# Sparse attention's gate projection: weights stationary instead of x, and its place among the first matmuls of the layer

## The chip, the core and the metric

The kernel runs on one core of one Trainium2 chip. The metric is the device time of one execution in microseconds (us). Engines are named as in the profile: PE is TensorE's matmuls and PEld its weight loads, DVE is VectorE, ACT is ScalarE, POOL is GpSimd, SP is SyncE, which here only issues DMAs.

## The reference, cut to what matters

A model of three blocks on 256 tokens of width 1024: the first has two mixers, cross attention and an FFN, the other two each an FFN, a mixer and an FFN. The mixer of the second block is sparse attention ("nsa"). Of it, this is what the change touches:

```python
hn = rmsnorm_2(x, mix_norm[layer])            # x: 256 tokens x 1024
...
q, kc, vc, ks, vs, kw, vw, gates = jnp.split(h @ w_in, splits, axis=-1)
...
g = jax.nn.sigmoid(gates.reshape(B, S, NSA_HKV, G, 3).transpose(0, 2, 3, 1, 4))
o = g[..., 0:1] * o_cmp + g[..., 1:2] * o_sel + g[..., 2:3] * o_win
```

`gates` are the last 48 columns of the 2608 of `w_in`: for each of 16 query heads three numbers per token, one for each of the three kinds of attention. Everything is float32.

## The kernel before, in words

**Layout.** The residual stream `HT` is kept transposed: the 1024 features in eight blocks of 128 partitions, the 256 tokens along the free axis. The input of a projection, x, is `XR`: the same eight blocks, scaled by the norm's gain, each split into a high part (rounded to the matmul's fp32r) and a low part (the rest). Weights come from memory in units of 2048 columns (eight k-blocks of 256 output features), and are split likewise into `WH` and `WL`. ScalarE writes the high part (L1152), VectorE the low part (L1737). There are three buffers for raw and three for split units. `mm2` (L511) makes one product of three matmuls: high times high, and the two mixed ones. The root of the mean square is not applied to x but afterwards, to the results (`scale`, L1770, on VectorE, with rows `RN`, or with a column per token).

**A unit.** `unit_T` (L536) computes a unit of 256 features: its weights are stationary (128 x 128), x moves (256 columns), and the result comes out transposed as features x tokens. It is 2 halves x 8 blocks x 3 = 48 matmuls. The gate is the exception (L966 to L973): its unit has 8 x 48 columns, and there x is stationary and the weights move, 48 columns at a time, so that the result has tokens on its partitions: 2 halves of the tokens x 8 blocks x 3 = 48 matmuls also. The later steps want it so: `gates` is a per-token, per-head factor (`settle_pair`, L1889, and the compressed part).

**Order.** Each engine runs a list written out by hand, and they meet at semaphores. The order around the change is, on TensorE: the last matmuls of the FFN's output; the gate (first the six blocks of x that are there, then the seventh and eighth; `in_order_of_x`, L532); the column sums for the norm (`norm_sum`, L588: two matmuls of 256 columns and four of 2, in a bank of their own); unit 6 (first keys, `("k", 0)`); unit 0 (first queries); the sum of squares of the first keys (`sum_squares`, L688, one float32 matmul of 512 columns, two in the records); unit 8; the next sum; unit 7; the next; and then the loop of `p` in 0 to 18 over pairs of heads (L997), in which each step has scores, transposes and weighted sums, with the other units between. Its last steps (about 932 to 966 us) are thin: small matmuls between exponentials and reductions.

On ScalarE (L1577 to L1600): the high part of unit 0 (`asked(("nsa_gate", 0))`, which looks three units ahead), the root of the mean square (`rsqrt_mean`, L1178, two operations), the high part of unit 8 (`asked(("nsa_w_in", 6))`), the gate's three steps (exponential twice, logarithm, exponential, L1582 to L1588), the squares of the first keys (`nsa_square`), the high part of unit 7, the root for them (`nsa_root`), and so on. A high part waits until the unit that held its buffer three before has been used: unit 8 follows the gate, unit 7 follows unit 6.

On VectorE (L2320 on): the low part of unit 0, `ncol`, the low part of unit 8, the scaling of the first keys, the low part of unit 7, the scaling of the first queries, and so on. The last block of x is written at L1745 (`chunk_lo`), after the FFN's last result has been added at L1795.

PSUM has eight banks. `take("main", ...)` goes round banks 0 to 2, `take("aux", ...)` round 4 to 7; each waits for the event named by `empties` of its former holder. `RS` is half of ScalarE's scratch, 512 columns; `in_bank` gives the bank of a key.

Of the kernel before, what the change touches and what calls it, by code (L numbers as in the profile page):

```python
# [194 lines left out]
def program(nc, A, out):  # L195
# [5 lines left out]
    ACT = mybir.ActivationFunctionType  # L201
# [4 lines left out]
    U = {name: u for u, (name, *_) in enumerate(UNITS)}  # L206
# [12 lines left out]
    with ctx:  # L219
# [3 lines left out]
        def signal(name, step=1):  # L223
            s = Signal(ctx.enter_context(nc.semaphore("s_" + name)), step)
            SIGNALS.append(s)
            return s
# [33 lines left out]
        SQ, RS, T2 = TMP[:, 0, :], TMP[:, 1, :], TMP[:, 2, :]  # L260
# [6 lines left out]
        used = signal("used")  # L267
# [10 lines left out]
        cmp_pe = signal("cmp_pe")  # L278
# [6 lines left out]
        copied = signal("copied")  # L285
        sig1 = signal("sig1")
# [16 lines left out]
        lo_done = signal("lo")  # L303
        parts = signal("parts")
        rscaled = signal("rscaled")
# [38 lines left out]
        def stat(name, n):  # L344
            if name not in stat_of:
                stat_of[name] = stat_at[0]
                stat_at[0] += n
                assert stat_at[0] <= 768, "STAT"
            return STAT[:, stat_of[name]:stat_of[name] + n]
# [6 lines left out]
        def tiles(ap, t):  # L356
            return ap.rearrange("p (k t) -> p k t", t=t)
# [11 lines left out]
        def con(name):  # L369
            at, n = CCOLS[name]  # L370
            return CON[:, at:at + n]

        def half(buf, n):
            return buf[:, n * 512:n * 512 + 512]

        def two(buf):
            return tiles(buf[:, 0, :], 256), tiles(buf[:, 1, :], 256)

        def split_at(u, cols):

            if u in IN_XR:
                return XR[:, 0, 0:cols], XR[:, 1, 0:cols]
            return WH[:, PART[u], 0:cols], WL[:, PART[u], 0:cols]
# [5 lines left out]
        ident, ones64, ones128 = con("ident"), con("ones64"), con("ones128")  # L389
# [67 lines left out]
        gates = stat("gates", 96)  # L457
# [5 lines left out]
        def in_bank(key):  # L463
            return banks[BANK[key]][:, :]
# [25 lines left out]
        def tensor(e, counting):  # L490
            q = Queue(e, counting)
# [5 lines left out]
            def take(kind, key):  # L497
                i = kinds[kind][turn[kind] % len(kinds[kind])]
                turn[kind] += 1
                for s, k in emptied.pop(i, ()):  # L500
                    q.wait_ge(s, k)
                BANK[key] = i
                return banks[i]

            def empties(key, *events):
                emptied[BANK[key]] = events

            def mm(o, l, r, start=True, stop=True):
                return e.matmul(o, l, r, start=start, stop=stop)  # L509

            def mm2(o, l, r, start, stop):  # L511
                mm(o, l[0], r[0], start, False)
                mm(o, l[0], r[1], False, False)
                return mm(o, l[1], r[0], False, stop)

            def at_k(x, k, a, n):
                return x[0][:, k, a:a + n], x[1][:, k, a:a + n]

            def weights(name, n=256, cols=2048):
                u = U[name]  # L520
                _, _, _, whole = UNITS[u]
                if whole:
                    q.wait_ge(raw[u % NRAW], u)
                    return u, tiles(RAW[:, u % NRAW, 0:cols], n)
                q.wait_ge(lo_done, u)
                return u, tuple(tiles(part, n) for part in split_at(u, cols))
# [5 lines left out]
            def in_order_of_x(m, k):  # L532

                return (0, m, k) if k < 6 else (k, m, k)

            def unit_T(name, x, x_name, pieces, *events, kind="main", order=in_time):  # L536
                u, w = weights(name)
                b = take(kind, name)
                for m, k in sorted(((m, k) for m in range(2) for k in range(8)), key=lambda mk: order(*mk)):
                    q.wait_ge(parts, (x_name, k * pieces // 8))  # L540
                    t = mm2(b[:, m * 256:m * 256 + 256], at_k(w, k, m * 128, 128), at_k(x, k, 0, 256), k == 0 and m == 0, k == 7 and m == 1)
                t.then_inc(used.tick(u), 1)
                empties(name, *events)
# [144 lines left out]
            def sum_squares(key, ones, *events, squares=SQ):  # L688
                b = take("aux", key)
                q.wait_ge(squared, key)  # L690
                mm(b[:, :], ones, squares).then_inc(summed.tick(key), 1)
                empties(key, *events)


            xT = two(XR)
# [192 lines left out]
            def nsa_unit(i, key, kind="one"):  # L888
                unit_T(("nsa_w_in", i), xT, "mix_0", 8, (rscaled, key), kind=kind)
# [12 lines left out]
            def nsa_sum(key):  # L902
                sum_squares(key, ones64, (ln_done, key))
# [59 lines left out]
                    t = mm(b[:, r * 256:r * 256 + 256], BDV[:, G, r, :], PCT[:, G, :], False, r == 1)  # L963
                t.then_inc(cmp_pe.tick(("out", G)), 1)

            name = ("nsa_gate", 0)  # L966
            u, w = weights(name, 48, 384)
            b = take("main", name)
            for j, k in sorted(((j, k) for j in range(2) for k in range(8)), key=lambda jk: in_order_of_x(*jk)):
                q.wait_ge(parts, ("mix_0", k))  # L970
                t = mm2(b[:, j * 48:j * 48 + 48], at_k(xT, k, j * 128, 128), at_k(w, k, 0, 48), k == 0 and j == 0, k == 7 and j == 1)
            t.then_inc(used.tick(u), 1)
            empties(name, (sig1, ("gate", 1)))  # L973
            norm_sum("mix_0")
            nsa_unit(6, ("k", 0), "main")
            nsa_unit(0, ("q", 0), "main")
            nsa_sum(("k", 0))
            nsa_unit(8, ("k", 1), "main")
            nsa_sum(("q", 0))
# [116 lines left out]
            for p in range(11):  # L1096
# [18 lines left out]
                if 0 <= p - 3:  # L1115
# [6 lines left out]
                    b = in_bank(("diff", "o", h // 2))  # L1122
# [15 lines left out]
        def scalar(e, counting):  # L1138
            q = Queue(e, counting)
# [14 lines left out]
            def asked(name, less=0):  # L1154
                ahead(U[name] + NW - less)
# [22 lines left out]
            def rsqrt_mean(stage):  # L1178

                n = 260 if stage in WITH_COLS else 256  # L1180
                b, r = in_bank(("norm", stage)), RN[stage][:, 0:n]
                q.wait_ge(small["con"], 0)
                q.wait_ge(ssq, stage)
                if stage == "ffn1_0":
                    e.activation(RR, b[:, 0:256], ACT.Ln, bias=eps, scale=0.125).then_inc(ln_done.tick("final"), 1)
                    q.wait_ge(ln_done, "final")
                    e.activation(r, RR, ACT.Exp, scale=-1.0).then_inc(rstd.tick("final2"), 1)
                    q.wait_ge(cols, "final")
                    e.activation(r, r, ACT.Ln, bias=eps, scale=0.125).then_inc(ln_done.tick("final2"), 1)
                    q.wait_ge(cols, "final2")  # L1190
                    e.activation(r, r, ACT.Exp, scale=-0.5).then_inc(rinv.tick(stage), 1)
                    e.activation(RR, RR, ACT.Exp, scale=-0.5).then_inc(rstd.tick("final"), 1)
                    return
                e.activation(r, b[:, 0:n], ACT.Ln, bias=eps, scale=0.125).then_inc(ln_done.tick(stage), 1)
                q.wait_ge(ln_done, stage)
                e.activation(r, r, ACT.Exp, scale=-0.5).then_inc(rinv.tick(stage), 1)
# [12 lines left out]
            def copy(key, dst, src):  # L1209
                e.activation(dst, src, ACT.Copy).then_inc(copied.tick(key), 1)  # L1210
# [10 lines left out]
            def rows_square(key, src, dst, former):  # L1221

                if former is not None:
                    q.wait_ge(summed, former)
                e.activation(dst, src, ACT.Square).then_inc(squared.tick(key), 1)
# [314 lines left out]
            def nsa_square(key):  # L1540
                q.wait_ge(rscaled, key)
                rows_square(key, half(QN, key[1]) if key[0] == "q" else (T2, KR1)[key[1]], SQ, FORMER_N[key] or ("ob2", 3))
# [33 lines left out]

            asked(("nsa_gate", 0))  # L1577
            rsqrt_mean("mix_0")
            asked(("nsa_w_in", 6))
            q.wait_ge(used, U[("nsa_gate", 0)])  # L1580
            q.wait_ge(cols, "ncol")
            for j in range(2):  # L1582
                e.activation(gates[:, j * 48:j * 48 + 48], in_bank(("nsa_gate", 0))[:, j * 48:j * 48 + 48], ACT.Exp,
                             scale=ncol[:, j:j + 1]).then_inc(sig1.tick(("gate", j)), 1)
            q.wait_ge(sig1, ("gate", 1))
            e.activation(gates, gates, ACT.Ln, bias=con("one")[:, 0:1]).then_inc(sig2.tick("gate"), 1)
            q.wait_ge(sig2, "gate")
            e.activation(gates, gates, ACT.Exp, scale=-1.0).then_inc(gated.tick("gate"), 1)  # L1588
            nsa_square(("k", 0))
            asked(("nsa_w_in", 0))  # L1590
            nsa_root(("k", 0))
            nsa_square(("q", 0))
# [1023 lines left out]
```

## Time and profile before

| | us |
|---|---|
| median of 3 runs | 1682.28 |
| lowest and highest of them | 1681.22, 1685.14 |
| the profiled execution | 1686.05 |
| its span in the profile | 1684.2 |
| PE busy, share of the span | 1652.2, 98% |
| DVE busy, share | 1095.1, 65% |
| ACT busy, share | 919.5, 55% |
| HBM read over the span | 281 MB, 167 GB/s |

The profile is of one execution. A matmul's length there contains the filling and emptying of the array, so matmuls that follow each other overlap; how long a run of them takes is read from the difference of starts. The granted clock is a share of TensorE's full speed: 1.00 is its level of 2.4 GHz and 0.50 its level of 1.2 GHz. Times in the text are counted from the span's start.

### The profile page before, as it was taken

To read this page: it belongs to the slowest core of one execution; us is meant where nothing else is said; L and a number is where in the kernel's file an instruction comes from. 1 tells how busy PE (TensorE), PEld (TensorE's weight loads), DVE (VectorE), ACT (ScalarE), POOL (GpSimd) and SP (SyncE) were. 2 spreads that over 40 slices of the span, in tenths; PEclk is the share of its full clock that TensorE was granted. 3 is DMA by queue.
4 is the path that set the end of the run, shared out by engine and by line. 5 is a ranking of instruction groups with operands and counts; after the bars stand their busy time and mean duration, and the time that the engine had idled before them with its cause. 6 is when DMAs were issued, how large, how long until landed. Compare 5 with 4: busy or idle time off the path is not lost.

```text
span 1684.2 us, 30435 instructions
## 1 busy us (share of the span) xinstructions
PE 1652.2 (98%) x13180; PEld 1566.1 (93%) x13180; DVE 1095.1 (65%) x1371; ACT 919.5 (55%) x1248; POOL 159.2 (9%) x63
## 2 busy tenths in 40 slices
PE   7999999999999999999999899999999999999999
PEld 7999989999999989998988699998999898799998
DVE  6888868664666567756578856656655667665554
ACT  6966778445444455434487844444443447754432
POOL 0000000000022101220000002210122000012210
PEclk9999999999999999999899899999999999999999
DMA  7555344454455455545542235545554564245543
GB/s 268 184 176 172 130 150 143 184 179 147 150 190 186 156 197 199 200 162 172 195 143 101 101 126 192 183 155 197 203 198 160 173 220 151 101 143 184 191 155 129
DMA packets 44629, 284.01 MB, mean 169 GB/s; under 512 B 4944, under 2 KB 6608, under 8 KB 17744
## 3 DMA queue, kind: packets, MB, share of 16 engines
q1 hardware_dynamic: 44352, 281.99, 48.0%
q8 instruction: 104, 1.70, 0.4%
q14 instruction: 29, 0.24, 0.0%
q10 hardware_dynamic: 144, 0.08, 0.0%
HBM read 281.00 MB, written 1.05 MB: 167 GB/s over the span
## 4 chain that ended last, share of the span: by engine, by line
PE 86%; DVE 6%; ACT 5%; issue 2%; DMA 1%; DVEq 0%; ACTq 0%
PE bank L509 85%; ACT WH L1152 2%; DVE WL L1737 2%; PE bank L660 1%; DVE HT L1793 0%; ACT SB L1275 0%; ACT XM L1159 0%; DVE XM L1745 0%; ACT XR L1159 0%; ACT FB L1176 0%; DVE FB L1763 0%; DVE STAT L1882 0%; DMA RAW<-in_nsa_w_out 0%; DMA PAR<-in_par 0%; DVE FA L2178 0%
## 5 line engine op out<-in xcount | busy, mean ns | idle before, releaser
L1737 DVE TENSOR_TENSOR WL<-RAW,WH 128x2048 fp32r<-128x2048 f32 (+1 forms) x282 | 590.3, 2096 | 272.2 <-ACT WH L1152 272.0
L509 PE MATMUL bank<-XR,WH 128*128 128x256 f32 x3648 | 651.2, 282 | 11.2 <-DVE WL L1924 10.7
L1152 ACT ACTIVATE WH<-RAW 128x2048 fp32r<-128x2048 f32 (+1 forms) x282 | 493.1, 1752 | 217.4 <-PE bank L509 211.2
L509 PEld LDWEIGHTS bank<-XR,WH 128*128 128x128 f32 x3648 | 559.7, 189 | 15.5 <-DVE WL L1924 10.7
L509 PE MATMUL bank<-XR,WL 128*128 128x256 f32 x1824 | 511.1, 280 | 0.0
L509 PEld LDWEIGHTS bank<-XR,WL 128*128 128x128 f32 x1824 | 344.4, 189 | 0.0
L509 PE MATMUL bank<-XF,WH 128*128 128x512 f32 x880 | 305.3, 392 | 0.0
L509 PE MATMUL bank<-XM,WH 128*128 128x256 f32 x1664 | 299.0, 282 | 3.3 <-DVE XM L1745 1.8
L509 PEld LDWEIGHTS bank<-XM,WH 128*128 128x128 f32 x1664 | 256.9, 190 | 4.8 <-DVE XM L1745 2.8
L509 PE MATMUL bank<-XF,WL 128*128 128x256 f32 x880 | 246.0, 280 | 0.0
L509 PE MATMUL bank<-XM,WL 128*128 128x256 f32 x832 | 234.2, 281 | 0.0
L509 PEld LDWEIGHTS bank<-XF,WH 128*128 128x128 f32 x880 | 165.2, 188 | 36.3
L2463 POOL TENSOR_TENSOR FA<-FA,R 128x512 f32<-128x512 f32 x33 | 92.2, 2794 | 859.7 <-ACT FA L1252 859.7
L509 PEld LDWEIGHTS bank<-XF,WL 128*128 128x128 f32 x880 | 165.2, 188 | 0.0
L509 PEld LDWEIGHTS bank<-XM,WL 128*128 128x128 f32 x832 | 157.7, 190 | 0.0
L1199 ACT ACTIVATE XF<-FA 128x512 fp32r<-128x512 f32 x55 | 34.8, 633 | 214.5 <-DVE FA L1837 214.5
L509 PE MATMUL bank<-WH,XR 128*128 128x256 f32 (+1 forms) x608 | 114.8, 287 | 0.3 <-ACT FA L1219 0.3
L2463 POOL TENSOR_TENSOR FA<-FA,FB 128x512 f32<-128x512 f32 x22 | 61.2, 2781 | 420.3 <-ACT FA L1252 420.3
L509 PEld LDWEIGHTS bank<-WH,XR 128*128 128x128 f32 x608 | 96.1, 192 | 2.2 <-issue 1.6
L509 PE MATMUL bank<-WL,XR 128*128 128x256 f32 (+1 forms) x304 | 86.0, 283 | 0.0
L1837 DVE TENSOR_TENSOR FA<-FA,bank 128x512 f32<-128x512 f32 x55 | 37.7, 686 | 69.6 <-PE bank L509 60.8
L1159 ACT ACTIVATE XR<-HT,PAR 128x256 fp32r<-128x256 f32 x40 | 19.6, 507 | 97.0 <-DVE HT L1795 78.3
(278 smaller groups left out, 1667.0 us busy)
## 6 DMA issues: line engine op xcount, KB each, us to landing
RAW<-in_f1i SPq DMA_DIRECT2D x44, 1024.0 KB, 4.9
RAW<-in_f2i SPq DMA_DIRECT2D x44, 1024.0 KB, 4.9
RAW<-in_w_in SPq DMA_DIRECT2D x35, 1024.0 KB, 4.9
RAW<-in_w_ffn_in SPq DMA_DIRECT2D x22, 1024.0 KB, 4.8
RAW<-in_f1o SPq DMA_DIRECT2D x32, 704.0 KB, 4.1
RAW<-in_f2o SPq DMA_DIRECT2D x32, 704.0 KB, 4.1
RAW<-in_diff_w_in SPq DMA_DIRECT2D x12, 1024.0 KB, 5.0
RAW<-in_w_ffn_out SPq DMA_DIRECT2D x16, 704.0 KB, 4.2
```

The lines of the kernel that those rows point to most:

```text
L509: return e.matmul(o, l, r, start=start, stop=stop)
L660: t = e.transpose(b[:, c * 128:c * 128 + 128], slot(name, i)[:, c * 128:c * 128 + 128], ident)
L1152: e.activation(split_at(u, cols)[0], RAW[:, u % NRAW, 0:cols], ACT.Copy).then_inc(hi_done.tick(u), 1)
L1159: e.activation(two(XN[stage])[0][:, k, :], src, ACT.Copy, scale=gain(stage, k)).then_inc(xhi.tick((stage, k)), 1)
L1199: e.activation(buf[:, 0, at:at + n], src, ACT.Copy).then_inc(xhi.tick(key), 1)
L1737: e.tensor_tensor(lo, RAW[:, u % NRAW, 0:cols], hi.bitcast(f32), sub).then_inc(lo_done.tick(u), 1)
L1837: e.tensor_tensor(p, p, in_bank((w_in, 11 + c))[:, :], mult).then_inc(ffn_mul.tick((stage, c)), 1)
L2463: e.tensor_tensor(tiles(half(F(4), c % 4), 256), tiles(half(F(3), c % 4), 256), r_of(stage), mult).then_inc(sr_done.tick((stage, c)), 1)
```

## The change

On TensorE the gate is computed with its weights stationary and x moving. The stationary block is 128 columns wide though the gate has 48, so rows 48 to 127 of the result are not used, and for the last block the columns behind the unit's end are what an earlier unit left. It is 8 blocks x 3 = 24 matmuls of 256 columns. It comes between the parts of unit 6: six blocks of unit 6, six of the gate, then the seventh of both, then the eighth of both. The column sums follow behind both. The result is copied out of its bank by ScalarE and turned back by two transposes behind unit 0. On ScalarE the copy comes before the high part of unit 8, and the squares of the first keys now come before the gate's exponentials.

```diff
-            name = ("nsa_gate", 0)
-            u, w = weights(name, 48, 384)
-            b = take("main", name)
-            for j, k in sorted(((j, k) for j in range(2) for k in range(8)), key=lambda jk: in_order_of_x(*jk)):
-                q.wait_ge(parts, ("mix_0", k))
-                t = mm2(b[:, j * 48:j * 48 + 48], at_k(xT, k, j * 128, 128), at_k(w, k, 0, 48), k == 0 and j == 0, k == 7 and j == 1)
-            t.then_inc(used.tick(u), 1)
-            empties(name, (sig1, ("gate", 1)))
+            def gate_columns(b, k0, k1):
+
+                u = U[("nsa_gate", 0)]
+                q.wait_ge(lo_done, u)
+                wh, wl = split_at(u, 464)
+                for k in range(k0, k1):
+                    q.wait_ge(parts, ("mix_0", k))
+                    at = slice(k * 48, k * 48 + 128)
+                    t = mm2(b[:, 0:256], (wh[:, at], wl[:, at]), at_k(xT, k, 0, 256), k == 0, k == 7)
+                if k1 == 8:
+                    t.then_inc(used.tick(u), 1)
+                    empties(("nsa_gate", 0), (copied, "gate"))
+
+            def gate_turn():
+                b = take("aux", "gate")
+                q.wait_ge(copied, "gate")
+                for j in range(2):
+                    t = e.transpose(b[:, j * 128:j * 128 + 128], RS[:, j * 128:j * 128 + 128], ident)
+                t.then_inc(cmp_pe.tick("gate"), 1)
+                empties("gate", (sig1, ("gate", 1)))
+
+            name = ("nsa_w_in", 6)
+            u, w = weights(name)
+            b, g = take("main", name), take("main", ("nsa_gate", 0))
+            for k0, k1 in ((0, 6), (6, 7), (7, 8)):
+                for m in range(2):
+                    for k in range(k0, k1):
+                        q.wait_ge(parts, ("mix_0", k))
+                        t = mm2(b[:, m * 256:m * 256 + 256], at_k(w, k, m * 128, 128), at_k(xT, k, 0, 256), k == 0 and m == 0, k == 7 and m == 1)
+                if k1 == 8:
+                    t.then_inc(used.tick(u), 1)
+                    empties(name, (rscaled, ("k", 0)))
+                gate_columns(g, k0, k1)
             norm_sum("mix_0")
-            nsa_unit(6, ("k", 0), "main")
             nsa_unit(0, ("q", 0), "main")
+            gate_turn()
             nsa_sum(("k", 0))
...
             asked(("nsa_gate", 0))
             rsqrt_mean("mix_0")
+            q.wait_ge(used, U[("nsa_gate", 0)])
+            copy("gate", RS[:, 0:256], in_bank(("nsa_gate", 0))[:, 0:256])
             asked(("nsa_w_in", 6))
-            q.wait_ge(used, U[("nsa_gate", 0)])
+            nsa_square(("k", 0))
             q.wait_ge(cols, "ncol")
+            q.wait_ge(cmp_pe, "gate")
             for j in range(2):
-                e.activation(gates[:, j * 48:j * 48 + 48], in_bank(("nsa_gate", 0))[:, j * 48:j * 48 + 48], ACT.Exp,
+                e.activation(gates[:, j * 48:j * 48 + 48], in_bank("gate")[:, j * 128:j * 128 + 48], ACT.Exp,
                              scale=ncol[:, j:j + 1]).then_inc(sig1.tick(("gate", j)), 1)
             q.wait_ge(sig1, ("gate", 1))
...
-            nsa_square(("k", 0))
             asked(("nsa_w_in", 0))
             nsa_root(("k", 0))
```

Nothing changes on VectorE, GpSimd or in the order of the DMAs.

## Rows read from the trace of the kernel before

**Rows 1.** The page, part 4: shares of the chain that ended last, by engine.

```profile
PE 86%; DVE 6%; ACT 5%; issue 2%; DMA 1%; DVEq 0%; ACTq 0%
```

**Rows 2.** The chain of waits, 812 to 866 us: start, us, what.

```profile
811.92 54.17 PE bank L509 x388
```

**Rows 3.** Stretches: length, busy PE, PEld, DVE, ACT, POOL; granted clock, DMA, GB/s.

```profile
817.42:820.30 2.88, 2.88 (x29) 2.88 (x27) 2.19 (x5) 1.36 (x3) 1.34 (x2) 1.00 0.38 108
820.30:830.50 10.20, 10.20 (x47) 10.02 (x47) 4.32 (x5) 5.18 (x8) 0.72 (x1) 0.50 0.65 242
857.00:932.00 75.00, 73.80 (x628) 63.25 (x626) 59.57 (x164) 59.78 (x163) 0.00 (x0) 1.00 0.35 126
932.00:936.30 4.30, 1.99 (x24) 1.55 (x24) 4.08 (x15) 4.27 (x10) 0.00 (x0) 1.00 0.71 292
936.30:946.60 10.30, 9.57 (x66) 6.92 (x64) 9.12 (x32) 7.92 (x28) 0.00 (x0) 0.67 0.30 103
```

**Rows 4.** Timeline of TensorE: gate, column sums, unit 6 (start us, us, engine, line, operation).

```profile
817.42 0.19 PE L509 MATMUL bank<-WH,XR 128*128 128x48 f32 x1
...
824.60 0.39 PE L509 MATMUL bank<-WH,XR 128*128 128x48 f32 x1
824.81 1.20 PE L509 MATMUL bank<-FB,CON 128*128 128x256 f32 x2
...
826.52 0.77 PE L509 MATMUL bank<-XR,WH 128*128 128x256 f32 x2
```

**Rows 5.** Timeline of TensorE: three sums of squares, units 8 and 7 between.

```profile
839.68 1.02 PE L509 MATMUL bank<-TMP,CON 128*128 128x512 f32 x2
...
840.78 0.28 PE L509 MATMUL bank<-XR,WL 128*128 128x256 f32 x1
...
846.20 1.02 PE L509 MATMUL bank<-TMP,CON 128*128 128x512 f32 x2
...
852.73 1.02 PE L509 MATMUL bank<-TMP,CON 128*128 128x512 f32 x2
```

**Rows 6.** Timeline of ScalarE, 826 to 836 us.

```profile
826.70 0.48 ACT L1194 ACTIVATE R<-bank,CON 128x260 f32<-128x260 f32 x1 [4.93 <-PE bank L509]
...
827.53 1.89 ACT L1152 ACTIVATE WH<-RAW 128x2048 fp32r<-128x2048 f32 x1
829.33 0.47 ACT L1583 ACTIVATE STAT<-bank,STAT 128x48 f32<-128x48 f32 x2
...
830.24 0.28 ACT L1588 ACTIVATE STAT<-STAT 128x96 f32<-128x96 f32 x1
835.00 0.63 ACT L1225 ACTIVATE TMP<-TMP 128x512 f32<-128x512 f32 x1 [4.47 <-DVE TMP L1774]
```

**Rows 7.** Timeline of VectorE, 815 to 856 us.

```profile
815.82 2.29 DVE L1737 TENSOR_TENSOR WL<-RAW,WH 128x2048 fp32r<-128x2048 f32 x1 [3.33 <-ACT WH L1152]
...
819.56 0.49 DVE L1745 SCALAR_TENSOR_TENSOR XR<-HT,PAR,XR 128x256 fp32r<-128x256 f32 x1 [0.66 <-ACT XR L1159]
...
834.27 0.69 DVE L1774 TENSOR_TENSOR TMP<-bank,R 128x512 f32<-128x512 f32 x1 [2.53 <-PE bank L509]
...
855.18 0.75 DVE L2223 SCALAR_TENSOR_TENSOR FB<-FB,PAR,TMP 128x512 f32<-128x512 f32 x1 [1.92 <-ACT TMP L1234]
```

**Rows 8.** Timeline of TensorE: six transposes and what follows them.

```profile
867.92 0.87 PE L660 MATMUL bank<-CON,SB 128*128 128x128 f32 x6
868.55 0.48 PE L509 MATMUL bank<-XR,WH 128*128 128x256 f32 x2
```

**Rows 9.** Timeline of ScalarE: two copies out of a bank; first pair's weights.

```profile
855.05 0.82 ACT L1558 ACTIVATE FA<-bank,R 128x256 f32<-128x256 f32 x2
...
866.03 0.89 ACT L1284 ACTIVATE SB<-SB,STAT 128x256 f32<-128x256 f32 x2
```

**Rows 10.** Waits of TensorE, 932 to 966 us: for whom, us, times, longest.

```profile
PE bank L660 <- ACT FB L1284: 1.8, 1, 1.8
PE bank L509 <- DVE FB L2340: 1.8, 1, 1.8
```

## The prediction

> **What bounds the kernel now.** I read the page first. The chain that ended last is TensorE for 86% of the span [rows 1]. So I asked for that chain around the change: from 812 to 866 us it is one piece, TensorE matmuls without a wait [rows 2]. There a microsecond taken from TensorE is a microsecond of the kernel, until another engine comes late.
>
> Next, the stretches with their granted clock. From 817.42 us, where the gate begins, TensorE is busy all the time. For 2.88 us the clock is 1.00, its 2.4 GHz level; then, for 10.2 us, it is 0.50, its 1.2 GHz level [rows 3]. No idle time comes before this fall. The only other long stretch below full clock begins at 936.3 us, behind 4.3 us in which TensorE was busy for 1.99 [rows 3]. The timeline shows what ran at 820.3: the gate, 48 matmuls that move 48 columns each through 128 x 128 weights. Its first starts at 817.42, its last at 824.60, and the column sums at 824.81 [rows 4]. The 47 steps from first to last take 7.18 us: 2.88 at full clock and 4.30 at half, together 5.03 us of full clock, or 0.107 us each. A matmul with 256 columns takes hardly more, 0.118 us (46 of them between 840.78 and 846.20 [rows 5]). So 48 columns cost nearly what 256 do: something other than the moving columns sets the gate's pace, and the array is mostly empty meanwhile.
>
> **The change, part by part.** I add up TensorE from 817.42 to the third sum of squares, which starts at 852.73 [rows 5]: 35.3 us today.
>
> Start. The first work is now unit 6 instead of the gate. Its low part is written by VectorE from 815.82 for 2.29 us, to 818.11 [rows 7]; VectorE can't begin earlier. The gate's own weights were ready, so today nothing waits. With some 0.06 us for the semaphore TensorE starts at 818.17: 0.75 us lost. Only the last FFN matmuls covered it.
>
> Unit 6 and the gate. 48 + 24 = 72 matmuls at 0.118 are 8.5 us, to 826.65. The six-block order needs the last block of x at the earliest after 54 of them, at 824.5; VectorE has it at 819.56 + 0.49 = 820.05 [rows 7]. No wait on x before and none after, so the splitting of unit 6 into six, one and one blocks by itself gains nothing. The gate that is replaced took 7.39 us (817.42 to 824.81 [rows 4]); at full clock throughout it would have been 48 x 0.107 = 5.1.
>
> Column sums. They took 824.81 to 826.52 [rows 4], 1.71 us at half clock, and should take 0.86 at full. They issue until 827.5, and their end is 0.14 later, 827.65, against 826.66 today.
>
> Unit 0. 48 x 0.118 = 5.66 us, to 833.17. Two transposes behind it: six take 0.63 us [rows 8], so two take 0.21; I take 0.25. Their input, the copy, is long there (next step). TensorE reaches the sum of the first keys' squares at 833.42.
>
> A new wait. That sum waits for a chain which used to be hidden behind units 6 and 0 and now has only unit 0. From the sums' end: root on ScalarE, 826.70 to 827.53, 0.83 us [rows 6]; the copy, 0.41 (two took 0.82 [rows 9]); the high part of unit 8, 1.90 [rows 6]; its low part, 2.29 [rows 7]; the scaling, 0.69 [rows 7]; the squares, 0.63 [rows 6]. With 0.1 us of semaphores this is 6.85 us: 827.65 becomes 834.5. TensorE waits 1.1 us. Queued behind this wait are the sum, unit 8 and all later work of TensorE; nobody else needs them sooner. The transposes stand ahead of it and cost nothing while it lasts.
>
> The next sum. ScalarE then does the gate's three steps, 829.33 to 830.52 today, so 1.19 us [rows 6]; they used to fall into idle time, and now they precede the high part of unit 7. 834.5 + 1.19 + 1.90 + 2.29 (low part) + 0.69 (scaling) + 0.63 (squares) = 841.2. TensorE: 834.55 + 0.86 for the sum (a sum and two matmuls take 1.10 us [rows 5], less 0.24) + 5.66 for unit 8 = 841.1. A wait of 0.2. The third sum's squares come by 846.7, and TensorE arrives at 841.3 + 0.86 + 5.66 = 847.8: no wait.
>
> Sum: 852.73 - 847.8 = **4.9 us earlier**. Checked another way. Gate, column sums and unit 6 took 817.42 to 834.0 today (839.68 less unit 0's 5.66), 16.6 us; at full clock they would take 5.1 + 0.86 + 5.66 = 11.6. So the clock gives 5.0. The gate's 24 matmuls in place of 48 give 5.1 - 2.8 = 2.3. Given back are 0.75 + 0.25 + 1.1 + 0.2 = 2.3. The sum is 5.0, and the change lives on the clock alone.
>
> Further on. VectorE and ScalarE gain less at first: the key normalization at 855.18 [rows 7] follows unit 1's low part, and by the same addition comes 4.0 us earlier. ScalarE's last weights of the first pair end at 866.92 [rows 9], then 862.9; the transposes that need them start at 867.92 [rows 8], then 863.0. It just fits, or costs 0.2. From 857 to 932 VectorE and ScalarE are busy 59.6 and 59.8 of 75 us [rows 3], so they catch up. In the thin part from 932 to 966 TensorE waits for both [rows 10], and they have started earlier too. Copy and DMAs: SyncE holds two small loads until the column sums, now 1 us later; what they bring (`CC`, `W2`) is used only in the last third of the loop. I keep 4.9, between 4.0 (VectorE's shift) and 6.0 (no new waits: 4.9 + 1.1 + 0.2, rounded down).
>
> The profiled execution took 1686.05 us, for a span of 1684.2; it becomes 1681.2. It stands 3.8 above the median of the runs, 1682.28, for which I forecast 1682.3 - 4.9 = **1677.4 us**. About 0.2% (3.4 us) is what a measurement of this kernel can tell from no change.
>
> **A rule against it.** In the rows the clock falls with TensorE fully busy [rows 3]. The Trainium skill (TensorE: Matmul & The Clock Gate, "Why this matters for your kernels") names idle gaps between bursts of matmuls as what makes it fall. By that rule the gate did not do it, the new order does not lift it, and its two new gaps of about 1 us could only hurt. That is the first rival below. Here the trace differs from the rule: 2.88 busy microseconds stand ahead of the fall.
>
> **Rivals.**
> 1. The change doesn't do what it says, since the clock's gain does not come: the fall at 820.3 isn't the gate's and recurs, or the timed runs mostly didn't have it (the profiled run's 3.8 us above the median would fit that). For: only one execution is seen. Against: the fall lies in the middle of the only narrow run of this kind. Then the 2.3 us of matmuls saved stand against the 2.3 given back, and the time is 1682.3. It is decided by whether the clock is at 0.50 anywhere from 817 to 834. Chance 0.22.
> 2. The thin part also profits. Its 10.3 us at clock 0.67 [rows 3] depend on how its gaps fall; shifted, it may keep more clock. At most half of 10.3 x 0.66 is 3.4 us: 1674.0. Nothing in the change favours it. Chance 0.05.
> 3. Slower. The thin part loses more: TensorE is busy 1.99 of 4.3 us there and waits 1.8 us twice [rows 3, 10]. If the engines, differently shifted, wait longer between 940 and 966 the clock falls there again and holds down the dense output units behind. One more such fall of 10.2 us costs 5.1 and leaves 1682.5, no difference; from the second on it is slower: 1677.4 + 10.2 = 1687.6. For: gaps are many; against: none is made longer by this change. One fall 0.03, two 0.04.
>
> **How the numbers follow.** The main case has 0.66. Its own range is 1675.9 to 1679.0: 4.0 to 6.0 us, and half a microsecond for the medians. The likeliest time is 1677.4. Eight in ten need part of rival 1 as well, so the range goes to 1682.5, just past that rival's time; below it ends at 1675.0, which takes in part of rival 2. Faster by over 0.2% (under 1678.9): the main case but for its slow edge, 0.63, and rival 2, 0.05: 0.68. Same: 0.22 + 0.03 + 0.03 = 0.28. Slower: 0.04.
>
> **What would show it.** In the timeline after: TensorE idle for about 0.75 us before unit 6; 72 matmuls at 0.118 us; clock 1.00 from 817 to 930; column sums in 0.86 us; waits of about 1.1 and 0.2 us before the first two sums of squares; unit 7's sum near 847.8. A clock of 0.50 anywhere in 817 to 850 makes the forecast wrong, as does a wait of more than 2 us before the first sum, which would mean ScalarE's order costs more than added up here.

## The result, and the profile after

The changed kernel takes 1677.42 us in the median of 13 runs (1671.93 to 1684.35), against 1682.28 for the kernel before in the 13 runs beside them. The ratio is 0.9971, with a 95% interval of 0.9959 to 0.9984: 4.9 us less, and between 2.7 and 6.9. The profiled execution took 1678.25 us. Runs of one kernel scatter by 2 to 5 us (standard deviation); most of what follows rests on the profiles, and on means over many runs.

The stretches of the profile after: the first from the end of the FFN's matmuls to the end of the column sums, the second to the third sum of squares, the third to 925 us, with the first part of the loop, the fourth its thin part. They answer to [rows 3]; columns as there.

```profile
816.34:826.43 10.09, 9.50 (x81) 9.29 (x79) 5.30 (x7) 2.84 (x3) 2.06 (x2) 1.00 0.51 188
826.43:846.45 20.02, 19.17 (x153) 18.01 (x153) 11.41 (x13) 14.88 (x22) 0.00 (x0) 1.00 0.53 174
846.45:925.00 78.55, 77.75 (x656) 66.38 (x656) 62.85 (x167) 62.66 (x167) 0.00 (x0) 1.00 0.38 137
925.00:965.00 40.00, 34.58 (x248) 26.09 (x245) 30.05 (x113) 29.63 (x93) 0.00 (x0) 0.79 0.18 65
```

Where the clock was 0.50 for 10.2 us [rows 3], it is 1.00 throughout, up to 925 us. The timeline of TensorE after, which answers to [rows 4, 5, 8]:

```profile
816.22 0.28 PE L509 MATMUL bank<-XF,WL 128*128 128x256 f32 x1
817.09 0.51 PE L509 MATMUL bank<-XR,WH 128*128 128x256 f32 x2 [0.59 <-DVE WL L1764]
...
825.63 0.60 PE L509 MATMUL bank<-FB,CON 128*128 128x256 f32 x2
826.07 0.50 PE L509 MATMUL bank<-CON,FB 128*128 128x2 f32 x4
826.43 0.48 PE L509 MATMUL bank<-XR,WH 128*128 128x256 f32 x2
...
832.12 0.38 PE L983 MATMUL bank<-CON,TMP 128*128 128x128 f32 x2
833.35 1.10 PE L509 MATMUL bank<-TMP,CON 128*128 128x512 f32 x2 [0.85 <-ACT TMP L1250]
...
839.88 1.06 PE L509 MATMUL bank<-TMP,CON 128*128 128x512 f32 x2
...
846.45 1.02 PE L509 MATMUL bank<-TMP,CON 128*128 128x512 f32 x2
```

The last FFN matmul starts at 816.22, and the next could start 0.12 later, at 816.34. It waits for unit 6's low part until 817.09. The 72 matmuls of unit 6 and the gate run to 825.63, at 0.119 us each. The column sums take 0.80 us. After unit 0 and the transposes TensorE waits for the squares (line 1250 is their line now). From 816.34 to the third sum of squares are 30.1 us; before they were 35.3 [rows 4, 5].

What was one piece of TensorE in the chain of waits [rows 2] is now this (start, us, what):

```profile
812.79 1.93 ACT WH L1177
...
814.75 2.30 DVE WL L1764
...
817.09 9.49 PE bank L509 x78
...
827.11 0.42 ACT R L1221
...
827.81 1.81 ACT WH L1177
...
829.64 2.29 DVE WL L1764
831.94 0.61 DVE TMP L1801
...
832.57 0.64 ACT TMP L1250
...
833.35 28.41 PE bank L509 x222
```

With the clock at 1.00, TensorE has two gaps, in which it waits for other engines: for the splitting of unit 6 ahead of its work, and for root, splitting of unit 8, scaling and squares behind it.

The spans of the two profiled executions differ by 7.7 us (1684.2 and 1676.5), more than the runs. By stretches, in us, from starts in each timeline, with the later profiles of both kernels beside them; the marks are the end of the FFN's matmuls before the gate, the third sum of squares, the last output unit of sparse attention (nsa), and that of the third block's attention (diff):

| profile | to the gate | to third sum | to last nsa unit | to last diff unit | to the end |
|---|---|---|---|---|---|
| before | 817.4 | 35.3 | 132.6 | 499.8 | 199.0 |
| before, second | 817.0 | 32.1 | 139.6 | 501.1 | 199.1 |
| change | 816.3 | 30.1 | 135.4 | 498.2 | 196.4 |
| change, second | 816.0 | 30.1 | 133.2 | 498.4 | 196.4 |
| change, third | 815.9 | 30.2 | 132.4 | 498.4 | 196.4 |

Only the column to the third sum is clearly the change's doing. The next one varies within one kernel by 7 us. The others are 0.7 to 2.9 us shorter in the change, where its matmuls are those of before; more on that at the end of this document.

### The profile page after: what moved, and what is told of

It is laid out like the page before. It is cut to its first block, busy times and chain, and to the rows that moved or that the text cites. A ratio compares the mean times of both kernels' runs of the same rounds, so it can differ in the third digit from the quotient of the medians.

```text
span 1676.5 us, 30391 instructions
## 1 busy us (share of the span) xinstructions
PE 1643.1 (98%) x13158; PEld 1556.2 (93%) x13158; DVE 1094.7 (65%) x1371; ACT 920.0 (55%) x1249; POOL 159.3 (10%) x63
## 4 chain that ended last, share of the span: by engine, by line
PE 85%; DVE 6%; ACT 5%; issue 2%; DMA 1%; SPq 0%; DVEq 0%; ACTq 0%
PE bank L509 84%; ACT WH L1177 3%; DVE WL L1764 2%; PE bank L660 1%; DVE HT L1820 0%; ACT SB L1300 0%; DMA RAW<-in_w_in 0%; DMA RAW<-in_nsa_w_in 0%; ACT XM L1184 0%; DVE XM L1772 0%; ACT FB L1201 0%; DVE FB L1790 0%; DVE STAT L1909 0%; DMA RAW<-in_nsa_w_out 0%; DVE FA L2205 0%
## 5 line engine op out<-in xcount | busy, mean ns | idle before, releaser
L509 PE MATMUL bank<-XM,WH 128*128 128x256 f32 x1664 | 294.8, 281 | 3.3 <-DVE XM L1772 1.8
L509 PE MATMUL bank<-WH,XR 128*128 128x256 f32 x576 | 107.4, 285 | 0.3 <-ACT FA L1244 0.3
L509 PEld LDWEIGHTS bank<-WH,XR 128*128 128x128 f32 x576 | 89.6, 189 | 2.2 <-issue 1.6
L509 PE MATMUL bank<-WL,XR 128*128 128x256 f32 x288 | 81.0, 281 | 0.0
```

## The experiments

The theory: a run of nothing but narrow matmuls makes the clock fall, and the change's gain is that fall. Rivals: the new order keeps the clock up; or the fall has another cause and comes and goes by itself.

**The kernel before, again.**

> The kernel before once more, for a second profile. Theory: the fall to 0.50 begins 2 to 6 us after the gate's start in this profile too, and holds for about 10 us. Rival: the gate runs at 1.00 in this execution, and the fall belongs to only some of them.

Measured: mean 1683.8 us of 10 runs. The stretches from the gate's start (817.01), to its end, over the column sums, and on to the third sum of squares at 849.11:

```profile
817.01:822.29 5.28, 5.28 (x51) 5.28 (x49) 3.90 (x7) 2.83 (x3) 2.06 (x2) 1.00 0.62 211
822.29:825.80 3.51, 3.51 (x17) 3.35 (x17) 1.56 (x2) 1.82 (x3) 0.00 (x0) 0.53 0.33 63
825.80:849.11 23.31, 23.31 (x190) 22.35 (x189) 13.29 (x13) 13.32 (x19) 0.00 (x0) 1.00 0.56 199
```

The whole gate ran at 1.00 here, in 5.3 us; the fall came right behind it, and lasted 3.4 us, not 10. Half of the expectation failed: the fall came, but its cost is 1.7 us here (half of its length; 30.4 of the 32.1 us are left for full clock), where the first profile's 10.2 us cost 5.1. Its place and length are a matter of the execution.

**The new place with the old operands.**

```diff
+            for k0, k1 in ((0, 6), (6, 7), (7, 8)):
+                ... unit 6, blocks k0 to k1, as in the change
+                for j in range(2):
+                    for k in range(k0, k1):
+                        t = mm2(g[:, j * 48:j * 48 + 48], at_k(xT, k, j * 128, 128), at_k(wg, k, 0, 48), k == 0 and j == 0, k == 7 and j == 1)
```

> The new place with the old operands: unit 6's six blocks, then the narrow gate's six blocks (36 matmuls of 48 columns in a row), then the rest; no copy, no transposes. Theory 'run of narrow matmuls': 36 of them take 3.9 us, longer than the 2.9 us that stood ahead of the fall before, so the clock falls again, to 0.50, and the time is that of before within 2 us. Rival 'the new order keeps the clock up': clock 1.00, about 3 us faster than before.

Measured: mean 1683.7 us of 10 runs, the kernel before beside it 1683.7 of 25; ratio 0.9995 (0.9968 to 1.0022). From the FFN's end to the third sum 37.7 us. The run of 36 narrow matmuls starts at 821.86:

```profile
821.86 0.18 PE L509 MATMUL bank<-WH,XR 128*128 128x48 f32 x1
...
824.35 0.53 PE L509 MATMUL bank<-WH,XR 128*128 128x48 f32 x2
824.70 0.39 PE L509 MATMUL bank<-WL,XR 128*128 128x48 f32 x1
```

and the stretches of this kernel, before, in and after that:

```profile
817.58:821.86 4.28, 4.28 (x36) 4.28 (x37) 2.90 (x6) 2.84 (x3) 2.07 (x2) 1.00 0.68 251
821.86:825.50 3.64, 3.64 (x31) 3.64 (x30) 1.61 (x1) 0.00 (x0) 0.00 (x0) 0.85 0.31 54
825.50:835.50 10.00, 10.00 (x46) 9.82 (x46) 0.17 (x1) 1.42 (x3) 0.00 (x0) 0.50 0.25 94
```

The clock is 1.00 over the first six blocks of unit 6, all wide matmuls, and falls within the narrow run, at about 824.4, with TensorE busy all the time. It stays down for 13.7 us, which is why this stretch is longer than in either profile of before:

```profile
824.40:838.10 13.70, 13.70 (x64) 13.52 (x64) 1.46 (x2) 3.74 (x7) 0.00 (x0) 0.50 0.38 123
```

The mean granted clock of the timed runs was that of before (0.9924, against 0.9919 beside it). The new order alone does not keep the clock up.

**The same narrow matmuls, each alternating with one of unit 6.**

```diff
+                for n, (i, z) in enumerate(((0, 0), (0, 1), (1, 0))):
+                    t6 = mm(o, l[i], r[z], first and n == 0, last and n == 2)
+                    t = mm(og, lg[i], rg[z], first and n == 0, last and n == 2)
```

> The narrow gate as before (x stationary, 48 columns move, no copy, no transposes), but each of its matmuls alternates with one of unit 6. The same matmuls as before in another order. Theory 'a run of narrow matmuls alone makes the clock fall': clock stays 1.00, 96 matmuls in about 11 us, 32.4 us to the third sum, 3 us faster than before. Rival 'fewer TensorE instructions is what helps': as before, 35 us.

```profile
818.38:829.26 10.88, 10.88 (x97) 10.88 (x97) 4.51 (x6) 2.83 (x3) 2.06 (x2) 1.00 0.58 194
829.26:849.80 20.54, 19.83 (x156) 18.62 (x156) 11.87 (x14) 15.13 (x21) 0.00 (x0) 1.00 0.54 174
```

Clock 1.00; 96 matmuls in 10.9 us (11 expected); 32.2 us to the third sum (32.4 expected). In the timed runs 2.2 us under before by the means (1682.4 of 10, 1684.6 of 35), ratio 0.9988 (0.9969 to 1.0008): the sign fits, the times alone don't show it. The mean granted clock of these runs was 0.9943, against 0.9917 of before beside them.

**Wide matmuls added beside the narrow ones.**

```diff
                 t = mm2(b[:, j * 48:j * 48 + 48], at_k(xT, k, j * 128, 128), at_k(w, k, 0, 48), k == 0 and j == 0, k == 7 and j == 1)
+                for n in range(1 + j):
+                    mm(extra[:, 0:256], wh[:, k * 48:k * 48 + 128], xT[0][:, k, :])
```

> The kernel before with 24 matmuls of 256 columns added among the 48 narrow ones, into a bank that nobody reads. Theory 'narrow matmuls let the clock fall': work is added and yet the clock stays 1.00: gate 8.0 us, 33.2 us to the third sum, 2 us faster than before. Rival 'the clock's fall has another cause': the fall stays and the added work costs 2.8 to 5.6 us, slower than before.

```profile
817.41:825.61 8.20, 8.20 (x75) 8.20 (x74) 5.29 (x7) 2.84 (x3) 2.06 (x2) 1.00 0.48 143
825.61:850.69 25.08, 25.08 (x204) 24.07 (x203) 13.45 (x14) 15.14 (x21) 0.00 (x0) 1.00 0.53 189
```

24 matmuls more than before, and the clock stays: 33.3 us to the third sum (33.2 expected). Mean 1680.7 of 10 runs against 1683.7 of 25, ratio 0.998 (0.9962 to 0.9997), with a mean clock of 0.9952 against 0.9919. Added, useless work makes the kernel faster, by 0.5 to 6.4 us. This is the most direct evidence of the four, as nothing else of the kernel before was touched. Each of the four has one profile, and a fall's length varies; that the fall is gone, or still there, in the other runs rests on their mean clocks. What it is in a narrow matmul that lets the clock fall was not tested.

**The operands exchanged, in the old place.**

```diff
+            g = take("main", ("nsa_gate", 0))
+            gate_columns(g, 0, 8)
+            norm_sum("mix_0")
+            nsa_unit(6, ("k", 0), "main")
```

> The operands exchanged alone, in the gate's old place, column sums and unit 6 behind it. Theory 'the narrow gate sets the clock': clock stays 1.00, no idle start, about 1 us of waits on the last block of x and on the squares' sum: 29.6 us to the third sum of squares, 5.7 us faster than before, 0.5 faster than the change. Rival 'the order keeps the clock up': the clock falls here as before, 35 us.

```profile
815.92:845.75 29.83, 28.90 (x230) 27.31 (x229) 16.71 (x20) 17.84 (x25) 2.06 (x2) 1.00 0.49 176
```

Measured: 29.8 us to the third sum (29.6 expected), clock 1.00, waits of 0.49 us ahead of the column sums and 0.40 ahead of the second sum of squares, mean 1678.2 of 10 runs, ratio 0.9966 (0.9943 to 0.9989). The exchange alone is the whole gain. Putting the gate inside unit 6 adds nothing, as the blocks of x are nearly there in time: TensorE starts on the last of them 0.2 us late (at 818.60, where the matmul before it starts at 818.27 and the usual step is 0.12).

**The change again, and a version made from the sum.** What the change gives back, by the late start and the wait for the squares, can be saved: the gate, whose weights are there first, goes first; the column sums stand between the halves of unit 6, so that root and splitting begin earlier; the transposes go ahead of unit 0, and the gate's exponentials again ahead of the squares.

```diff
+            gate_columns(g, 0, 6)
+            unit_6(0, 0, 6)
+            gate_columns(g, 6, 8)
+            unit_6(0, 6, 8)
+            norm_sum("mix_0")
+            unit_6(1, 0, 8)
+            gate_turn()
+            nsa_unit(0, ("q", 0), "main")
```

> The changed kernel once more, for a second profile. All theories: TensorE's clock 1.00 from the gate's place to 925 us, and 30.1 us from the start of unit 6's place (the end of the FFN's matmuls) to the third sum of squares. Theory 'clock of the gate': 4 to 6 us faster than before in the timed runs. Theory 'the thin part takes part of it back': the stretch from 925 to 970 us differs between profiles of the same kernel by 1 to 4 us, with its clock.

> Wide gate first, then unit 6 in two halves with the column sums between them, the transposes ahead of unit 0 and the gate's exponentials ahead of the squares. If my sum of what the change gives back is right (0.75 us start, 1.1 us and 0.2 us of waits), these go: 28.5 us from the end of the FFN's matmuls to the third sum of squares against 30.1, so 1.7 us faster than the change and 6 to 7 us faster than before. Rival, that ScalarE and VectorE bound this stretch anyway: same as the change.

> The changed kernel in the same call as the three others, as their yardstick: locally 30.1 us; 5 to 6 us faster than before in the mean of the runs.

> The version with the sums between, again, to tell it from the change in the timed runs: 28.2 us locally as in its first profile; 1.9 us faster than the change if nothing further on takes it back, 0 if the thin part does.

The stretch of the new version in its second profile, from the FFN's end to the third sum of squares:

```profile
816.90:845.10 28.20, 28.20 (x231) 27.19 (x230) 18.48 (x21) 18.48 (x25) 2.06 (x2) 1.00 0.62 210
```

28.2 us in both its profiles (28.5 expected), TensorE busy in all of it; 30.1 and 30.2 for the change. Side by side on one chip the means were 1677.7 against 1679.2 (12 runs each), and 1675.3 (9 runs) against 1677.8 (11). Over all runs: version 1676.7 (21 runs, standard error 0.7), change 1678.2 (36, 0.5), before 1683.4 (the 119 of the experiments, 0.4). All four profiles show the 1.9 us; in the time they are likely, at 1.5 +- 0.9. The version's ratios to before are 0.9965 (0.9944 to 0.9985) and 0.997 (0.9956 to 0.9983): the lowest mean here, though the runs don't tell it from the exchange alone (0.9966). The change again gave 0.9973 (0.9955 to 0.9992) and 0.9979 (0.9966 to 0.9993); side by side it was 5.3 and 4.3 us under before in the means, the second time less than the 5 to 6 expected.

**Filling the thin part.** 32 unread matmuls were put ahead of waits in the loop's last steps, in the change and in the new version; then 10 of them, in the new version.

```diff
+            def fill(b, n):
+
+                for _ in range(n):
+                    mm(b[:, 384:512], ident, ones64)
...
                     b = take("aux", (name, "t", i))
+                    if name == "nsa" and p >= 9 and i == 2 * p:
+                        fill(b, 2)
```

> The changed kernel with 32 unread float32 matmuls of 128 columns (0.21 us each at full clock, 6.8 us together) in the thin part of the loop, ahead of waits. Theory 'the clock's fall in the thin part, 7 to 31 us long in the profiles so far, is what makes executions of one kernel differ and hides part of the gain': the clock from 925 to 970 us rises from 0.76 to 0.92 towards 0.97 or more, and the time falls by 1 to 4 us against the change, with less scatter than its 3 us. Rival 'the thin part is bound by ScalarE and VectorE, the clock is of no account there': the time stays, or rises by up to 6.8 us.

> The same filling in the version with the column sums between the halves of unit 6 and the transposes ahead of unit 0. If both effects are real they add: 1.5 to 2 us faster than e8, 8 to 11 us faster than before. If the loop's pace is set by ScalarE and VectorE from its first step on, it equals e8.

> The version with the sums between, with 10 unread matmuls (2.1 us at full clock) instead of 32, all between 922 and 940 us, where the clock falls first. Theory 'the filling costs what it adds where TensorE is the bound, and pays only in its waits': the first fall is avoided or later (clock from 925 to 945 us 0.9 or more, against 0.5 to 0.7), and the time is 0 to 2 us under that of the version without filling, 7 to 9 us under before. Rival 'every unread matmul costs its own time there': 2 us above it.

The thin part, 925 to 965 us, in the second profile of before, in the third of the change, and in the change filled:

```profile
925.00:965.00 40.00, 37.01 (x219) 26.94 (x217) 30.26 (x115) 27.27 (x88) 0.00 (x0) 0.62 0.24 92
```

```profile
925.00:965.00 40.00, 34.76 (x274) 27.12 (x272) 29.69 (x112) 29.36 (x91) 0.00 (x0) 0.87 0.16 62
```

```profile
925.00:965.00 40.00, 36.80 (x288) 29.43 (x287) 30.67 (x114) 29.08 (x93) 0.00 (x0) 0.87 0.19 70
```

The filling moved the fall without preventing it: the clock over these 40 us is 0.87 with and without it, where 0.97 was expected over 925 to 970. In the timed runs the mean clock of the whole kernel rose from 0.9945 to 0.9970, but the mean time did not fall by 1 to 4 us: it was 1679.0 us (12 runs) against 1677.8 (11), a difference of 1.2 +- 1.0. Ratio to before 0.9985 (0.9972 to 0.9997). In the new version the filled kernel took 1677.6 us (11 runs) against 1675.3 (9), 2.3 +- 1.1 more, with a ratio of 0.9976 (0.9961 to 0.999): 4.5 us under before, not 8 to 11. With 10 matmuls the clock from 925 to 945 us was 0.74, where 0.9 or more was expected, and the mean 1678.6 against 1676.7 over all runs of that version, ratio 0.9973 (0.9957 to 0.9989). That is the rival's 2 us, but its two sides ran on different chips, with an error of 1.1.

Clock and time do go together: over the 119 runs of before their correlation is -0.90. Scatter is less clear. It fell from 2.9 to 1.6 us with the filling in the change, and rose from 2.0 to 2.6 in the new version. As an estimate, 0.0025 of 1680 us are 4.2 us of clock won in the change; as the time rose by 1.2 all the same, the 6.8 us of added matmuls cost some 5. No filling that pays was found.

## Why the prediction was right, point by point

The time was forecast as 1677.4 and measured as 1677.42. With 3 us of scatter the last digits are luck. The parts are not.

- **Start, 0.75 us.** Measured 0.75 (816.34 to 817.09).
- **72 matmuls, 8.5 us.** Measured 8.54.
- **The old gate at full clock, 5.1 us.** It took 5.28 in the second profile of before.
- **Column sums, 0.86 at full clock.** Measured 0.80.
- **Transposes, 0.25, and the wait for the squares, 1.1.** From 832.12 to 833.35 are 1.23 us, 1.0 of it wait. The chain summed to 6.85 us from the end of the column sums; it took 6.78 (826.57 to 833.35).
- **The second wait, 0.2.** It wasn't there: 833.35 to 839.88 is 6.53, the same as a sum and a unit before. My chain for ScalarE and VectorE was 0.2 us too long: it summed to 6.70 from squares to squares and took 6.51 (833.20 to 839.71). I added durations end to end, but some operations begin up to 0.1 us before their predecessor's recorded end, as the high part of unit 7 here, at 834.21, behind an exponential recorded until 834.30.
- **Sum, 4.9 us by the third sum of squares.** Measured 5.2 (35.3 less 30.1).
- **That the clock is all of it.** Confirmed within the noise. The mean granted clock of the timed runs was 0.9921 before (119 runs) and 0.9949 in the change (36 runs); 0.0028 of 1680 us are 4.7 us of full clock, +- 0.7, where the means side by side differ by 4.8, 5.3 and 4.3 us. With the narrow run kept in the new place it stayed at 0.9924; with the narrow matmuls alternating it was 0.9943, with wide ones among them 0.9952, with the exchange alone 0.9952. Another sum agrees, as an estimate: the means less what the clock cost (13.3 and 8.6 us) are 1670.1 us before and 1669.6 in the change, so fewer matmuls and new waits come to about nothing, as forecast.
- **The fall of 10.2 us** was read from one execution, and this is the weak step. The second profile shows 3.4 us. Had that one been the first, the same working would have forecast 1.7 us from the clock and 1680.6. How long the fall is on the average, the clock of the runs tells, if the thin part loses the same in both kernels: 4.7 us lost is a fall of 9.4. That the first profile lay near this average is luck.
- **The rule against it.** Idle time does stand ahead of the fall in the thin part [rows 3], as the Trainium skill (TensorE: Matmul & The Clock Gate, "Why this matters for your kernels") says. But TensorE was busy without a gap right ahead of the falls at the gate and of the one in the narrow run above, and the idle 0.59 and 0.85 us of the change did not bring the clock down. The measurement decides: a run of narrow matmuls is enough.
- **Rival 1, the clock's gain doesn't come.** It is refuted: three profiles of the change have 1.00 there.
- **Rivals 2 and 3, the thin part gains or loses.** The mechanism is real and I had it too small and too one-sided. I read the fall there to 946.6 only; it went on to 950.1, so that 5.1 us of full clock were lost in it, not 3.4:

```profile
936.30:950.10 13.80, 13.07 (x86) 9.30 (x84) 12.13 (x42) 9.53 (x32) 0.00 (x0) 0.63 0.22 77
```

From 925 to 975 us the clock was 0.90 and 0.69 in the two profiles of before, 0.83, 0.86 and 0.90 in those of the change: 5 and 15 us lost, then 9, 7 and 5. The stretch that holds it took 132.6 and 139.6 us in the kernel before, and 135.4, 133.2 and 132.4 in the change. It belongs to the execution; that the change shifts it isn't shown.

## What to carry to other kernels

A matmul that moves few columns can cost twice: once because it takes nearly as long as a wide one (0.107 us for 48 columns here, 0.118 for 256), and again because the clock can fall to half in or behind a run of such matmuls, here for 3.4 to 13.7 us, and the dense work behind pays. Exchanging the operands, even at the price of a copy and two transposes, kept the clock up here, and so did mixing the narrow matmuls with wide ones. And when the clock's state matters, read it from several profiles or from the clock of all runs; of two executions of one kernel, one had a fall three times as long as the other's.

## What the runs showed of the hardware that was not expected

Outside the change the profiles differ by the pace of dense matmuls too, with the granted clock at 1.00. In the last FFN's input stage, three matmuls of 256 columns start every 360.0 ns in both profiles of before, and about every 352 in all three of the change. Two timelines there, the one matmul with low-part weights in each three, before and then after:

```profile
1540.33 0.28 PE L509 MATMUL bank<-XM,WL 128*128 128x256 f32 x1
...
1540.69 0.28 PE L509 MATMUL bank<-XM,WL 128*128 128x256 f32 x1
...
1541.05 0.28 PE L509 MATMUL bank<-XM,WL 128*128 128x256 f32 x1
```

```profile
1540.30 0.28 PE L509 MATMUL bank<-XM,WL 128*128 128x256 f32 x1
...
1540.65 0.28 PE L509 MATMUL bank<-XM,WL 128*128 128x256 f32 x1
...
1541.00 0.28 PE L509 MATMUL bank<-XM,WL 128*128 128x256 f32 x1
```

The pace keeps within a nanosecond or two over the stage, and takes one of few values: 352, 356 (in the alternating and in the exchanged-only kernel) or 360 ns. It is 2.6 us over that stage, the difference in the last column of the table. It isn't tied to the gate: the version with 10 filling matmuls, which has the exchanged gate, had 360.0 there too, and the kernel with the narrow gate in the new place did not. What sets it was not found.

Repeated profiles of one kernel agree in it (before twice, the change three times, the version with the sums between twice), so it may go with the program and be a part of what the timed runs compare. Those leave little room for it. The kernel with wide matmuls added had 352 in its profile where before had 360, and yet its mean less the clock's cost is 1672.7 us against 1670.1. This is an estimate; the 2.6 us between them are about the 2.8 of its 24 added matmuls, and nothing is won back by the pace.
